# One float32 kernel of three layers: squares added on VectorE ahead of the norms' sums, v's norm scaled in another order, and short unread products in layer 2

## The chip, the core and the metric

The program runs on one core of one Trainium2 chip. The metric is the device time of one execution in microseconds, the median of the runs shown. Besides the timed runs one execution was profiled; its span runs from the first to the last instruction of the program.

## What is computed

Three different layers act one after the other on 1024 tokens with 1024 features, all in float32. Layer 1 is a chunkwise mLSTM with a pooling branch and a squared-ReLU MLP; layer 2 adds 16 meta tokens and runs a wide causal convolution beside an attention of 8 heads; layer 3 has a gated branch whose values are normed and mixed in chunks of 128 tokens, beside a gated linear attention. Cut to what the change touches:

```python
def layer_norm(x, g, b):                       # layer 1, after the mixer (norm 1)
    mu = xf.mean(-1, keepdims=True)
    var = jnp.square(xf - mu).mean(-1, keepdims=True)
    return ((xf - mu) * lax.rsqrt(var + LN_EPS) * g + b)

x = layer_norm(ALPHA * x + mix, ln1_g[l], ln1_b[l])
...
# layer 3: v is layer-normed over its 1024 features (a_ln_g, a_ln_b, eps 1e-6), then mixed over tokens
# layer 2: rms_norm of c_q and c_kv, queries, keys and values from them, then block-causal attention
```

## The kernel before, in words

**Layout.** Features lie on the 128 partitions in 8 rows of 1024 tokens, tokens along the free dimension. `res[:, m, :]` is row m of the residual, `M[g]` row g of v in layer 3. A mean over features is a sum over partitions and rows: `ones` (128x128) times a row, accumulated over the rows in a PSUM bank.

**Products.** Every large product splits both factors in a rounded part and a rest (`hi`, `lo`) and adds three products, hi·hi, hi·lo and lo·hi (L270 to L272 in `Core.product`, L324 to L326 in `Core.three`). One step of such a generator is three matmuls of 128x512. Weights come in tiles of 8 blocks: SyncE loads `w_raw`, ScalarE casts it to `w_hi` (`Core.cast`, L131), GpSimd subtracts to get `w_lo` (`Core.pool`, four instructions of 128x256 a tile), with three buffers each. A cast waits until TensorE has used up the tile three back.

**Order.** Nothing is scheduled by the hardware: each engine runs its own list of instructions in order and waits on semaphores. `Lane.settle` makes an engine wait for its own last instruction. `advance(fill, n)` puts n steps of a product between two steps of a norm on TensorE, and `label(name)` notes which products were finished by then. ScalarE and VectorE handle those products at the same names, with `act_products(name)` and `dve_products(name)`. So the place of such a call in an engine's list sets what stands behind the wait for that product.

**The norms.** `HalfNorm` norms 512 tokens at a time, u counting the halves: u = 0, 1 are norm 1 (after `w_out`, in `Ffn1.pe_norm`, `act_norm`, `dve_norm`), u = 2, 3 norm 2, u = 4, 5 the norm of v in layer 3 (`Mixer3.pe_sgu`, `act_sgu`, `dve_sgu`). The order is: TensorE sums `total`; ScalarE makes the mean; VectorE subtracts it from eight rows (`dve_centre`); ScalarE squares each row into one of two or three buffers (`act_square`); TensorE adds each square by `ones` in plain float32 (`pe_square`, one matmul instruction that the profile shows as two records); ScalarE makes Ln and Exp of the sum (`root_guess`); VectorE corrects by a Newton step (`root_newton`, four instructions) and scales the rows. In norm 1 the fill between two squares is 2 steps, and 5 steps come before the first. The fill of half 0 is the second half of `w_out` (64 steps, a product each 8), that of half 1 the first hidden rows of `w_ff1` (32 steps), whose squared ReLU goes to and fro between ScalarE and VectorE. In norm 1 VectorE centres all eight rows and only then handles the products that were finished during the squares. In v's norm the 16 squares have 2 steps between them, out of an 80-step fill (`lr`, `u3` 0, `s3` 0, `u3` 1, `s3` 1, 16 steps each); both halves' roots follow, then eight scalings of half 0, then of half 1, and ScalarE adds the shift to each and copies the turned v (`vt_ready`) after all sixteen.

**Layer 2's start** (`Mixer2.pe`): TensorE makes gate and a products and the latents c 3, 4, `rot`; sums for the rms of the keys' latents (`kv rms`); latents c 0 to 2; sums for the queries' (`q rms`); more gates; then values, keys and queries from the normed latents; then the first head's scores.

Of the kernel before, what the change touches and what calls it, by code (L numbers as in the profile page):

```python
# [441 lines left out]
class HalfNorm:  # L442


    def __init__(self, core):
        self.k = core
        s = core.s
        self.total, self.summed, self.mean = s("norm_total"), s("norm_summed"), s("norm_mean")
        self.centred, self.square, self.squares_summed = s("norm_centred"), s("norm_square"), s("norm_squares_summed")
        self.guess, self.scaled = s("norm_guess"), s("norm_scaled")  # L450

    def pe_sum(self, t, u, total):
        i = u % 2
# [8 lines left out]
    def act_mean(self, a, u, mean):  # L462
        a.wait_ge(self.summed, u + 1)
        a.act(mean, self.k.ps[:, 4 + u % 2, :], ACT.Copy, scale=1.0 / D, inc=self.mean)

    def act_square(self, a, u, k, x, squares):
        n = len(squares)
        a.wait_ge(self.centred, 8 * u + k + 1)
        a.wait_ge(self.squares_summed, 8 * u + max(k - n + 1, 0))
        a.act(squares[k % n], x, ACT.Square, inc=self.square)  # L470

    def dve_centre(self, v, u, k, x, mean):
# [1 line left out]
        v.tt(x, x, mean, ALU.subtract, inc=self.centred)  # L474

    def act_guess(self, a, u, root, eps):
        a.wait_ge(self.squares_summed, 8 * u + 8)
# [484 lines left out]
class Ffn1:  # L962
# [146 lines left out]
    def pe_norm(self, t, u, squares, fill, n, name):  # L1109

        i = u % 2
        self.norm.pe_sum(t, u, self.total[:, 512 * i:512 * i + 512])
        advance(fill, n[0])
        self.k.label(("sum " + name, i))
        advance(fill, n[1])
        self.k.label(("mean " + name, i))
        for c in range(8):
            advance(fill, n[1])
            self.k.label(("square " + name, i, c))
            self.norm.pe_square(t, u, c, squares[c % 3])  # L1120
        for c in range(8):
            advance(fill, n[2])
            self.k.label(("apply " + name, i, c))
# [99 lines left out]
    def act_norm(self, a, u, squares, mean, root, name, eps, apply):  # L1223
        i, cols = u % 2, slice(512 * (u % 2), 512 * (u % 2) + 512)
        self.norm.act_mean(a, u, mean)
        self.act_products(a, ("sum " + name, i))
        self.act_products(a, ("mean " + name, i))
        self.norm.act_square(a, u, 0, self.k.real(0)[:, cols], squares)
        for c in range(8):
            if c < 7:  # L1230
                self.norm.act_square(a, u, c + 1, self.k.real(c + 1)[:, cols], squares)
# [109 lines left out]
    def dve_norm(self, v, u, mean, root, tmp, name, gain, eps, split):  # L1341
# [4 lines left out]
        self.dve_products(v, ("mean " + name, i))  # L1346
        for c in range(8):
            self.norm.dve_centre(v, u, c, x(c), mean)
        for c in range(8):
            self.dve_products(v, ("square " + name, i, c))  # L1350
        v.settle()
        self.norm.dve_root(v, u, root, tmp, eps)
        self.norm.dve_scale(v, u, 0, x(0), gain, root)
# [83 lines left out]
class Mixer2:  # L1437
# [196 lines left out]
    def pe_ones(self, t, key, total, stream, value, inc):  # L1634
# [4 lines left out]
        t.wait_ge(stream, value)  # L1639
        t.mm(k.ones_of(total, THREE, range(p.first, p.first + 3)), inc)  # L1640

    def pe_in(self, t, key, cols):
        drain(self.k.product(t, key, [block_of("w_in_2", c, cols) for c in range(8)], self.k.hi, self.k.lo, THREE,
                             lambda c, i: [(self.ffn.x2_ready, (8 if i else 0) + c + 1)]))
        self.k.label(key)
# [196 lines left out]
    def pe(self, t):  # L1842
# [8 lines left out]
            self.pe_in(t, ("c", i), 1024 + i * P)  # L1851
        self.pe_in(t, ("rot",), [(64, 1664, 32), (96, 1680, 16), (112, 1664, 16)])
        self.pe_ones(t, ("kv rms",), self.comp_total, self.row_total, 1, self.rms_sum)
        for i in (0, 1, 2):
            self.pe_in(t, ("c", i), 1024 + i * P)
        self.pe_ones(t, ("q rms",), self.comp_total, self.row_total, 3, self.rms_sum)
        for c in (2, 3):
            self.pe_gate(t, c)
        advance(branch, self.early_taps())
        k.label("latents")  # L1860
        drain(self.pe_values(t))
        drain(self.pe_keys(t, 0))
        drain(self.pe_queries(t, 0))
        k.label("heads")
        for i in self.SCORE_AT.values():
            self.pe_score(t, 0, i)
        for p in range(3):
# [669 lines left out]
class Mixer3:  # L2537
# [116 lines left out]
    def pe_sgu(self, t):  # L2654
# [10 lines left out]
        self.norm.pe_sum(t, 5, self.total[:, 512:1024])  # L2665
        advance(fill, self.FILL_V)
        k.label("v3 sum")
        for u in (4, 5):
            advance(fill, self.FILL_NORM)
            k.label(("v3 mean", u))  # L2670
            for g in range(8):
                advance(fill, self.FILL_NORM)
                k.label(("v3 square", u, g))
                self.norm.pe_square(t, u, g, self.T[3 + g % 2][:, 0:512])
        advance(fill, 48 - self.FILL_TOTAL - self.FILL_V - 18 * self.FILL_NORM)
        k.label("v3 gate")
        advance(fill, 16)
        k.label("v3 normed")
        for g in range(8):
            vt = self.vt[g % 2]  # L2680
            for half in range(2):
                t.wait_ge(self.v_normed, 8 * half + g + 1)
                t.wait_ge(self.vt_ready, 2 * g + half - 1)
                t.mm([(ps[:, 6 + half, i * P:(i + 1) * P], self.M[g][:, (4 * half + i) * P:(4 * half + i + 1) * P], k.ident[:, :], True, True)
                      for i in range(4)], self.vt_turned, transpose=True)
# [134 lines left out]
    def act_sgu(self, a):  # L2820
        k, ps = self.k, self.k.ps
        self.act_products(a, "v3")
        for u in (4, 5):
# [2 lines left out]
                self.act_products(a, "v3 sum")  # L2826
            self.act_products(a, ("v3 mean", u))
            for g in range(8):
                self.norm.act_square(a, u, g, self.M[g][:, 512 * (u - 4):512 * (u - 3)], [self.T[3][:, 0:512], self.T[4][:, 0:512]])
                self.act_products(a, ("v3 square", u, g))  # L2830
        for u in (4, 5):
            self.norm.act_guess(a, u, self.root[:, 512 * (u - 4):512 * (u - 3)], EPS)
        for u in (4, 5):
            cols = slice(512 * (u - 4), 512 * (u - 3))
            for g in range(8):
                a.wait_ge(self.norm.scaled, 8 * u + g + 1)
# [149 lines left out]
    def dve_sgu(self, v):  # L2986
# [7 lines left out]
        for u in (4, 5):  # L2994
            cols = slice(512 * (u - 4), 512 * (u - 3))
            self.dve_products(v, ("v3 mean", u))
            for g in range(8):
                self.norm.dve_centre(v, u, g, self.M[g][:, cols], self.mean[:, cols])
                self.dve_products(v, ("v3 square", u, g))
        for u in (4, 5):  # L3000
# [3 lines left out]
            for g in range(8):  # L3004
                self.norm.dve_scale(v, u, g, self.M[g][:, cols], "a_ln_g_3", self.root[:, cols])
            if u == 4:
                self.dve_products(v, "v3 gate")
        self.dve_products(v, "v3 normed")
        for g in range(8):
            r = g % 2  # L3010
            self.dve_products(v, ("sgu", g))
# [474 lines left out]
```

## Time and profile before

| | us |
|---|---|
| median of 3 runs | 3557.8 (3557.28 to 3564.66) |
| the profiled execution, its own time | 3553.04 |
| its span | 3550.9 |
| granted TensorE clock, mean | 0.98 |

| engine | busy, us | share of the span |
|---|---|---|
| PE (TensorE matmul) | 3397.2 | 96% |
| PEld (weight loads) | 2781.4 | 78% |
| DVE (VectorE) | 1778.6 | 50% |
| ACT (ScalarE) | 1119.2 | 32% |
| POOL (GpSimd) | 1087.9 | 31% |

Times inside the execution are from the start of the span. Of the chain that ended last, 81% is on PE and 13% on DVE. The span's 2.1 us difference to the execution's own time lies outside the instructions. Norm 1 lies at 437 to 531 us, layer 2's start at 1290 to 1475, v's norm at 2732 to 2797. An entry of a timeline may merge several instructions of one kind (x8); an instruction can start before the one ahead of it has ended.

### The profile page before, as it was taken

What the parts mean: (1) busy time and instruction counts of PE and PEld (TensorE: products, weight loads), DVE (VectorE), ACT (ScalarE), POOL (GpSimd) and SP (SyncE); (2) the same over time, 40 slices, a digit from 0 to 9 for tenths busy, and PEclk for the clock granted to TensorE, in tenths of its full rate; (3) what the DMA queues carried; (4) which work ended last, traced back from release to release, by engine and by line L of the source; (5) the groups of instructions that cost most, each with busy time, mean ns of one, the idle gap of its engine ahead of it and who ended that gap; (6) DMA issues with size and microseconds to landing.
All of it is one profiled execution on the core that took longest, in us unless ns stands there. A gap on an engine that the chain in (4) does not pass through costs nothing.

```text
span 3550.9 us, 39250 instructions
## 1 busy us (share of the span) xinstructions
PE 3397.2 (96%) x16240; PEld 2781.4 (78%) x16240; DVE 1778.6 (50%) x1897; ACT 1119.2 (32%) x1493; POOL 1087.9 (31%) x1144
## 2 busy tenths in 40 slices
PE   8998999999999999898799999999999999999997
PEld 6665768888888688555499999999987788888776
DVE  4666563222223578777547546446474423444532
ACT  4443352111112532444533111111142533333442
POOL 3111344222333333100014334334334222222253
PEclk9999999999999999899899999999999999999998
DMA  3000311111111221000021111111113111011242
GB/s 126 24 26 28 107 66 64 49 48 48 48 48 49 71 90 36 24 7 7 6 78 42 48 48 48 48 48 44 48 41 110 51 66 54 30 36 35 78 142 95
DMA packets 56249, 192.21 MB, mean 54 GB/s; under 512 B 6900, under 2 KB 7284, under 8 KB 55560
## 3 DMA queue, kind: packets, MB, share of 16 engines
q1 hardware_dynamic: 56072, 189.71, 15.4%
q8 instruction: 128, 2.10, 0.2%
q14 instruction: 49, 0.40, 0.0%
HBM read 172.83 MB, written 16.86 MB: 53 GB/s over the span
## 4 chain that ended last, share of the span: by engine, by line
PE 81%; DVE 13%; ACT 4%; issue 1%; DMA 0%; POOL 0%; DVEq 0%; ACTq 0%; SPq 0%; POOLq 0%
PE psum L270 21%; PE psum L271 21%; PE psum L272 21%; PE psum L138 11%; DVE mix L107 3%; DVE work L98 2%; PE psum L324 2%; PE psum L325 2%; PE psum L326 2%; DVE res L98 1%; DVE softmax_shift_columns L113 1%; PE psum L136 1%; DVE u_padded L98 1%; ACT L126 1%; DVE res L107 1%
## 5 line engine op out<-in xcount | busy, mean ns | idle before, releaser
L98 POOL TENSOR_TENSOR w_lo<-w_raw,w_hi 128x256 fp32r<-128x256 f32 x1140 | 1087.7, 986 | 2428.2 <-ACT w_hi L131 2428.2
L270 PE MATMUL psum<-x_hi,w_hi 128*128 128x512 f32 (+2 forms) x3240 | 1200.7, 371 | 12.6 <-DVE mix L98 5.9
L271 PE MATMUL psum<-x_lo,w_hi 128*128 128x512 f32 (+2 forms) x3240 | 1165.0, 360 | 0.0
L272 PE MATMUL psum<-x_hi,w_lo 128*128 128x512 f32 (+2 forms) x3240 | 1161.4, 358 | 0.0
L131 ACT CAST w_hi<-w_raw 128x1024 fp32r<-128x1024 f32 x285 | 298.3, 1048 | 1509.9 <-PE psum L272 1436.9
L270 PEld LDWEIGHTS psum<-x_hi,w_hi 128*128 128x128 f32 x3240 | 612.7, 189 | 104.1 <-issue 20.7
L271 PEld LDWEIGHTS psum<-x_lo,w_hi 128*128 128x128 f32 x3240 | 612.3, 189 | 82.1 <-issue 17.5
L272 PEld LDWEIGHTS psum<-x_hi,w_lo 128*128 128x128 f32 x3240 | 610.6, 188 | 70.2
L270 PE MATMUL psum<-h_hi,w_hi 128*128 128x512 f32 x824 | 325.2, 395 | 3.1 <-DVE res L98 3.1
L272 PE MATMUL psum<-h_hi,w_lo 128*128 128x512 f32 x824 | 320.8, 389 | 0.0
L271 PE MATMUL psum<-h_lo,w_hi 128*128 128x512 f32 x824 | 320.7, 389 | 0.0
L107 DVE SCALAR_TENSOR_TENSOR res<-res,psum 128x1024 f32<-128x1024 f32 (+1 forms) x88 | 90.3, 1026 | 238.5 <-PE psum L272 229.3
L270 PEld LDWEIGHTS psum<-h_hi,w_hi 128*128 128x128 f32 x824 | 154.7, 188 | 37.8 <-DVE res L98 3.6
L271 PEld LDWEIGHTS psum<-h_lo,w_hi 128*128 128x128 f32 x824 | 154.7, 188 | 34.2 <-issue 2.6
L272 PEld LDWEIGHTS psum<-h_hi,w_lo 128*128 128x128 f32 x824 | 154.6, 188 | 32.3
L138 PE MATMUL psum<-res 128*65 128x256 f32 (+5 forms) x480 | 167.3, 433 | 8.0 <-ACT res L131 4.2
L98 DVE TENSOR_TENSOR h_tmp<-h_tmp 128x1024 f32<-128x1024 f32 (+1 forms) x36 | 55.1, 1532 | 237.5 <-ACT h_tmp L126 237.5
L107 DVE SCALAR_TENSOR_TENSOR mix<-u_padded,vectors,mix 128x1044 f32<-128x1044 f32 x120 | 168.6, 1405 | 5.0 <-ACT work L131 0.8
L98 DVE TENSOR_TENSOR up<-psum,ffn_rms 128x1026 f32<-128x1026 f32 x44 | 54.0, 1226 | 191.0 <-PE psum L272 189.3
L324 PE MATMUL psum<-x_hi,w_hi 128*128 128x348 f32 (+2 forms) x328 | 129.8, 396 | 18.2 <-DVE x_lo L98 9.0
L107 DVE SCALAR_TENSOR_TENSOR up_conv<-up,vectors,up_conv 128x1024 f32<-128x1024 f32 x88 | 143.7, 1633 | 3.1
L98 DVE TENSOR_TENSOR res<-res,psum 128x1024 f32<-128x1024 f32 (+1 forms) x56 | 68.5, 1224 | 140.8 <-PE psum L272 135.7
(281 smaller groups left out, 3727.2 us busy)
## 6 DMA issues: line engine op xcount, KB each, us to landing
w_raw<-w_dram SPq DMA_DIRECT2D x285, 512.0 KB, 3.2
res<-spill SPq DMA_DIRECT2D x4, 1044.0 KB, 9.6
res<-x_dram SPq DMA_DIRECT2D x8, 512.0 KB, 8.9
res<-x_dram SPq DMA_DIRECT2D x4, 1024.0 KB, 8.0
spill<-res SPq DMA_DIRECT2D x1, 4096.0 KB, 13.9
spill_a<-mix SPq DMA_DIRECT2D x8, 512.0 KB, 2.7
res<-spill_a SPq DMA_DIRECT2D x8, 512.0 KB, 4.6
x_plain<-spill SPq DMA_DIRECT2D x4, 1024.0 KB, 10.7
```

What stands on the lines that cost most here:

```text
L98: self.mark(self.e.tensor_tensor(out, a, b, op), inc)
L107: self.mark(self.e.scalar_tensor_tensor(out, a, s, b, op0, op1), inc)
L113: self.mark(self.e.tensor_reduce(out, a, AX.X, op, negate=negate), inc)
L126: self.mark(self.e.activation(out, a, func, bias=bias, scale=scale), inc)
L131: self.mark(self.e.copy(out, a), inc)
L138: ins = self.e.matmul(out, lhsT, rhs, start=start, stop=stop, skip_group_check=True)
L270: t.e.matmul(out, whi, xhi, start=k == 0, stop=False, skip_group_check=True)
L271: t.e.matmul(out, whi, xlo, start=False, stop=False, skip_group_check=True)
L272: ins = t.e.matmul(out, wlo, xhi, start=False, stop=last_k, skip_group_check=True)
L324: t.e.matmul(out, whi, xhi, start=first, stop=False, skip_group_check=True)
L325: t.e.matmul(out, whi, xlo, start=False, stop=False, skip_group_check=True)
L326: return t.e.matmul(out, wlo, xhi, start=False, stop=last, skip_group_check=True)
```

## The change

In norm 1 and v's norm (u = 0, 1, 4, 5) VectorE now adds squares into one row: seven adds in u = 0 and 4, so that TensorE sums once instead of eight times, and five adds in u = 1 and 5, so that it sums three times (`ADDED`). ScalarE writes the first square to the total's row and the others to two buffers. The adds stand between the centrings (`dve_add_square(c - 2)` behind centring c, from c = 3 on). In norm 1 the products finished during the squares are now handled between the centrings too, where all of them used to come after. The number of fill steps is the same; the sums stand behind all of that part's fill. In v's norm the sum of u = 4 stands among u = 5's fill (3 steps a row there), that of u = 5 at 54 steps instead of 46; 10 steps follow instead of 18. Ln and Exp of both halves are paired; both Newton steps come before any scaling; VectorE scales row by row, both halves of a row, each with a settle, and takes the fill's next product (`u3` 1) behind row 2. ScalarE takes `u3` 0 and `s3` 0 behind the Exps. In layer 2 `pe_idle` puts 16, 12, 12 and 12 matmuls of 128x128 in float32, whose result nobody reads, at four places: behind the `kv rms` sums, ahead of the `q rms` sums, ahead of the values, and ahead of the first scores.

```diff
 class HalfNorm:
+    ADDED = {0: 7, 1: 5, 4: 7, 5: 5}
+    def sums(self, u):
+        return sum(8 - self.ADDED.get(w, 0) for w in range(u))
+    def adds(self, u):
+        return sum(self.ADDED.get(w, 0) for w in range(u))
...
+    def pe_square_total(self, t, u, total, squares):
+        n = self.ADDED[u]
+        t.wait_ge(self.added, self.adds(u + 1))
+        t.mm([(self.k.ps[:, 6 + u % 2, :], self.k.ones[:, :], total, True, n == 7)], self.squares_summed)
+        for k in range(n + 1, 8):
+            self.pe_square(t, u, k, squares[k % 2])
+    def act_square_of(self, a, u, k, x, total, squares):
+        a.wait_ge(self.centred, 8 * u + k + 1)
+        a.wait_ge(self.squares_summed, self.sums(u))
+        a.wait_ge(self.added, self.adds(u) + max(k - 2, 0))
+        a.act(squares[k % 2] if k else total, x, ACT.Square, inc=self.square)
+    def dve_add_square(self, v, u, k, total, squares):
+        v.wait_ge(self.square, 8 * u + k + 1)
+        v.settle()
+        v.tt(total, total, squares[k % 2], ALU.add, inc=self.added)
...
@@ Ffn1.pe_norm
         for c in range(8):
             advance(fill, n[1])
             self.k.label(("square " + name, i, c))
-            self.norm.pe_square(t, u, c, squares[c % 3])
+        self.norm.pe_square_total(t, u, squares[2], squares)
@@ Ffn1.dve_norm
         for c in range(8):
             self.norm.dve_centre(v, u, c, x(c), mean)
-        for c in range(8):
-            self.dve_products(v, ("square " + name, i, c))
+            if c > 2:
+                self.norm.dve_add_square(v, u, c - 2, self.squares[2], self.squares)
+            if c:
+                self.dve_products(v, ("square " + name, i, c - 1))
+        self.dve_products(v, ("square " + name, i, 7))
+        for c in range(6, self.norm.ADDED[u] + 1):
+            self.norm.dve_add_square(v, u, c, self.squares[2], self.squares)
@@ Mixer2
+    def pe_idle(self, t, n):
+        for _ in range(n):
+            t.e.matmul(self.k.ps[:, 6, 0:P], self.k.ones[:, :], self.k.ident[:, :], start=True, stop=True, skip_group_check=True)
...
         self.pe_ones(t, ("kv rms",), self.comp_total, self.row_total, 1, self.rms_sum)
+        self.pe_idle(t, 16)
         for i in (0, 1, 2):
             self.pe_in(t, ("c", i), 1024 + i * P)
+        self.pe_idle(t, 12)
         self.pe_ones(t, ("q rms",), self.comp_total, self.row_total, 3, self.rms_sum)
...
         k.label("latents")
+        self.pe_idle(t, 12)
...
         k.label("heads")
+        self.pe_idle(t, 12)
@@ Mixer3.pe_sgu
             for g in range(8):
-                advance(fill, self.FILL_NORM)
+                advance(fill, self.FILL_NORM + u - 4)
                 k.label(("v3 square", u, g))
-                self.norm.pe_square(t, u, g, self.T[3 + g % 2][:, 0:512])
-        advance(fill, 48 - self.FILL_TOTAL - self.FILL_V - 18 * self.FILL_NORM)
+                if u == 5 and g == 2:
+                    self.norm.pe_square_total(t, 4, self.T[3][:, 512:1024], squares)
+        self.norm.pe_square_total(t, 5, self.T[4][:, 512:1024], squares)
         k.label("v3 gate")
-        advance(fill, 16)
+        advance(fill, 64 - self.FILL_TOTAL - self.FILL_V - 18 * self.FILL_NORM - 8)
...
-                t.wait_ge(self.v_normed, 8 * half + g + 1)
+                t.wait_ge(self.v_normed, 2 * g + half + 1)
@@ Mixer3.act_sgu
+        for i, cols in enumerate(halves):
+            a.wait_ge(self.norm.squares_summed, self.norm.sums(5 + i))
+            a.act(self.root[:, cols], ps[:, 6 + i, :], ACT.Ln, bias=k.tiny[:, 1:2], scale=1.0 / D)
+        a.settle()
+        for cols in halves:
+            a.act(self.root[:, cols], self.root[:, cols], ACT.Exp, scale=-0.5, inc=self.norm.guess)
+        self.act_products(a, "v3 gate")
...
@@ Mixer3.dve_sgu
                 self.norm.dve_centre(v, u, g, self.M[g][:, cols], self.mean[:, cols])
+                if g > 2:
+                    self.norm.dve_add_square(v, u, g - 2, self.T[u - 1][:, 512:1024], [self.T[3][:, 0:512], self.T[4][:, 0:512]])
                 self.dve_products(v, ("v3 square", u, g))
...
             self.norm.dve_root(v, u, self.root[:, cols], self.tmp[:, cols], EPS)
-            for g in range(8):
+        self.dve_products(v, "v3 gate")
+        for g in range(8):
+            for u in (4, 5):
+                cols = slice(512 * (u - 4), 512 * (u - 3))
+                v.settle()
                 self.norm.dve_scale(v, u, g, self.M[g][:, cols], "a_ln_g_3", self.root[:, cols])
-            if u == 4:
-                self.dve_products(v, "v3 gate")
-        self.dve_products(v, "v3 normed")
+            if g == 2:
+                self.dve_products(v, "v3 normed")
```

## Rows read from the trace of the kernel before

**Rows 1.** The page: busy time, share and instructions of the engines.
```profile
PE 3397.2 (96%) x16240; PEld 2781.4 (78%) x16240; DVE 1778.6 (50%) x1897; ACT 1119.2 (32%) x1493; POOL 1087.9 (31%) x1144
```

**Rows 2.** Timeline, PE, norm 1 half 0: start, duration, instruction, idle before.
```profile
442.91 1.02 PE L138 MATMUL psum<-h_plain,ones 128*128 128x512 f32 x2
...
444.47 0.39 PE L270 MATMUL psum<-x_hi,w_hi 128*128 128x512 f32 x1
444.70 0.39 PE L271 MATMUL psum<-x_lo,w_hi 128*128 128x512 f32 x1
...
445.16 1.02 PE L138 MATMUL psum<-h_plain,ones 128*128 128x512 f32 x2
```

**Rows 3.** Timeline, DVE, norm 1: centrings, half 0's last `w_out` product, a hidden row's rest.
```profile
439.00 5.50 DVE L98 TENSOR_TENSOR res<-res,h_plain 128x512 f32<-128x512 f32 x8 [1.92 <-ACT h_plain L126]
...
489.47 0.69 DVE L107 SCALAR_TENSOR_TENSOR res<-res,psum 128x512 f32<-128x512 f32 x1 [0.50 <-PE psum L272]
...
510.74 1.15 DVE L98 TENSOR_TENSOR h_lo<-h_tmp,h_hi 128x512 fp32r<-128x512 f32 x1 [0.68 <-ACT h_hi L131]
```

**Rows 4.** Timeline, DVE, 466 to 474 us, beside the POOL tile of rows 5.
```profile
470.74 1.23 DVE L98 TENSOR_TENSOR x_lo<-res,x_hi 128x512 fp32r<-128x512 f32 x1
```

**Rows 5.** Timeline, POOL, 434 to 545 us: a weight tile.
```profile
468.38 4.18 POOL L98 TENSOR_TENSOR w_lo<-w_raw,w_hi 128x256 fp32r<-128x256 f32 x4 [10.62 <-ACT w_hi L131]
```

**Rows 6.** Timeline, ACT, norm 1: Ln of half 0, a cast, Ln of half 1.
```profile
459.74 0.69 ACT L126 ACTIVATE h_plain<-psum,tiny 128x512 f32<-128x512 f32 x1 [3.12 <-PE psum L138]
...
507.58 1.05 ACT L131 CAST w_hi<-w_raw 128x1024 fp32r<-128x1024 f32 x1 [2.31 <-PE psum L272]
...
513.56 0.69 ACT L126 ACTIVATE h_plain<-psum,tiny 128x512 f32<-128x512 f32 x1 [1.02 <-PE psum L138]
```

**Rows 7.** Windows, PE: stretch, its length, busy (instructions), granted clock, DMA share, GB/s.
```profile
525.80:531.00 5.20, 5.20 (x12) 0.50 0.22 79
...
2790.00:2795.00 5.00, 3.84 (x21) 1.00 0.01 3
```

**Rows 8.** Waits of PE, 1270 to 1480 us, the longest four: total, times, longest.
```profile
PE psum L270 <- DVE mix L98: 5.3, 1, 5.3
PE psum L374 <- DVE x_lo L98: 3.9, 1, 3.9
PE psum L138 <- DVE work L98: 3.9, 1, 3.9
PE psum L138 <- ACT x_hi L131: 3.4, 1, 3.4
```

**Rows 9.** Windows, PE, behind the four holes of layer 2; columns as in rows 7.
```profile
1335.20:1339.90 4.70, 4.70 (x16) 0.50 0.12 49
...
1375.80:1380.90 5.10, 5.07 (x11) 0.50 0.30 103
...
1429.90:1435.50 5.60, 5.60 (x13) 0.50 0.28 94
...
1456.10:1473.00 16.90, 13.52 (x38) 0.50 0.00 0
```

**Rows 10.** Timeline, DVE, 1378 to 1390 us: VectorE after the queries' rms sums.
```profile
1384.58 1.25 DVE L98 TENSOR_TENSOR work<-squares 128x1044 f32<-128x1044 f32 x1 [2.84 <-ACT squares L126]
```

**Rows 11.** Timeline, PE, v's norm: its last square, and the first chunk mixing.
```profile
2776.56 1.02 PE L138 MATMUL psum<-res,ones 128*128 128x512 f32 x2
...
2797.06 2.05 PE L138 MATMUL psum<-res,work 128*128 128x128 f32 x16 [0.82 <-ACT work L131]
```

**Rows 12.** Timeline, DVE, v's norm half 1: Newton step's start, eight scalings.
```profile
2787.26 0.69 DVE L98 TENSOR_TENSOR work<-res 128x512 f32<-128x512 f32 x1
...
2789.91 5.39 DVE L107 SCALAR_TENSOR_TENSOR mix<-mix,vectors,res 128x512 f32<-128x512 f32 x8
```

**Rows 13.** Timeline, ACT, v's norm half 0: the table load between Ln and Exp.
```profile
2775.84 1.28 ACT L126 ACT_TABLE_LOAD   x1
```

More of the change, by code:

```diff
@@ L450, in __init__ @@
         self.guess, self.scaled = s("norm_guess"), s("norm_scaled")
+        self.added = s("norm_square_added")
     def pe_sum(self, t, u, total):
@@ L468, in act_square @@
         a.wait_ge(self.centred, 8 * u + k + 1)
-        a.wait_ge(self.squares_summed, 8 * u + max(k - n + 1, 0))
+        a.wait_ge(self.squares_summed, self.sums(u) + max(k - n + 1, 0))
         a.act(squares[k % n], x, ACT.Square, inc=self.square)
@@ L476, in act_guess @@
     def act_guess(self, a, u, root, eps):
-        a.wait_ge(self.squares_summed, 8 * u + 8)
+        a.wait_ge(self.squares_summed, self.sums(u + 1))
         self.k.root_guess(a, root, self.k.ps[:, 6 + u % 2, :], D, eps, self.guess)
@@ L1227, in act_norm @@
         self.act_products(a, ("mean " + name, i))
-        self.norm.act_square(a, u, 0, self.k.real(0)[:, cols], squares)
+        self.norm.act_square_of(a, u, 0, self.k.real(0)[:, cols], squares[2], squares)
         for c in range(8):
             if c < 7:
-                self.norm.act_square(a, u, c + 1, self.k.real(c + 1)[:, cols], squares)
+                self.norm.act_square_of(a, u, c + 1, self.k.real(c + 1)[:, cols], squares[2], squares)
             self.act_products(a, ("square " + name, i, c))
@@ L2667, in pe_sgu @@
         k.label("v3 sum")
+        squares = [self.T[3][:, 0:512], self.T[4][:, 0:512]]
         for u in (4, 5):
@@ L2828, in act_sgu @@
             for g in range(8):
[L2829 to L2834, printed above, removed]
-            for g in range(8):
-                a.wait_ge(self.norm.scaled, 8 * u + g + 1)
+                self.norm.act_square_of(a, u, g, self.M[g][:, 512 * (u - 4):512 * (u - 3)], self.T[u - 1][:, 512:1024],
+                                        [self.T[3][:, 0:512], self.T[4][:, 0:512]])
+                if u == 4:
+                    self.act_products(a, ("v3 square", u, g))
+                else:
+                    k.cast(a, k.at["v3 square", u, g][0])
+        halves = [slice(0, 512), slice(512, 1024)]
+        for i, cols in enumerate(halves):
[6 more added lines that the diff above has]
+        for g in range(8):
+            for i, cols in enumerate(halves):
+                a.wait_ge(self.norm.scaled, 32 + 2 * g + i + 1)
                 a.act(self.M[g][:, cols], self.M[g][:, cols], ACT.Identity, bias=k.column("a_ln_b_3", g), inc=self.v_normed)
@@ L2998, in dve_sgu @@
                 self.norm.dve_centre(v, u, g, self.M[g][:, cols], self.mean[:, cols])
+                if g > 2:
+                    self.norm.dve_add_square(v, u, g - 2, self.T[u - 1][:, 512:1024], [self.T[3][:, 0:512], self.T[4][:, 0:512]])
                 self.dve_products(v, ("v3 square", u, g))
+            for g in range(6, self.norm.ADDED[u] + 1):
+                self.norm.dve_add_square(v, u, g, self.T[u - 1][:, 512:1024], [self.T[3][:, 0:512], self.T[4][:, 0:512]])
         for u in (4, 5):
@@ L3003, in dve_sgu @@
             self.norm.dve_root(v, u, self.root[:, cols], self.tmp[:, cols], EPS)
-            for g in range(8):
+        self.dve_products(v, "v3 gate")
+        for g in range(8):
+            for u in (4, 5):
+                cols = slice(512 * (u - 4), 512 * (u - 3))
+                v.settle()
                 self.norm.dve_scale(v, u, g, self.M[g][:, cols], "a_ln_g_3", self.root[:, cols])
-            if u == 4:
-                self.dve_products(v, "v3 gate")
-        self.dve_products(v, "v3 normed")
+            if g == 2:
+                self.dve_products(v, "v3 normed")
         for g in range(8):
```

## The prediction

> **What bounds the kernel.** The page comes first: PE is busy for 96% of the span [rows 1], so work taken from TensorE counts one for one, unless another engine's chain takes its place where it stood. So next I read, for each edited stretch, the timelines of PE, DVE and ACT side by side and ask who is waited for at its end. In norm 1 half 0 TensorE goes without a pause: square, two fill steps, square [rows 2]. ScalarE's Ln waits for it [rows 6], VectorE has long centred all rows [rows 3]. TensorE is the bound there and VectorE has slack; the question is how much of it 7 or 5 adds use up. In layer 2 the list of PE's waits gives four holes of 5.3, 3.9, 3.9 and 3.4 us [rows 8], and the windows behind them show a granted clock of 0.50, which is 1.2 GHz instead of 2.4 [rows 9].
>
> **Prices.** Records of the split products start 0.23 us apart (444.47, 444.70), so a step of three takes 0.68. From square to square 2.25 us pass, of which two steps are 1.36: one square's sum costs 0.89 [rows 2]. The change drops 7 + 5 + 7 + 5 = 24 of them, 21.4 us of PE work. A centring takes 5.50 / 8 = 0.69 us [rows 3]; an add of the same shape, which waits for its own engine, I take at 0.72. Beside a working GpSimd the same form takes 1.23 [rows 4], and a weight tile's four subtractions last 4.2 us then [rows 5], so a tile costs a busy VectorE about 4 x 0.5 = 1.8 to 2 us.
>
> The Trainium skill says so too (GPSIMD Engine Reference, Key points): GpSimd shares its SBUF interfaces with VectorE and contends with instructions that have two SBUF inputs, as all the adds have. Without it half 0 below would end its adds about 3.5 us sooner.
>
> **Norm 1, half 0: about +1.0.** Without squares TensorE reaches the sum 8 x 0.89 = 7.1 us before 459.6, where it now ends the squares [rows 6], so at 452.5. VectorE: `dve_products("square", 1)` stands behind centring 2 and waits for the fill's first product, 13 steps before 452.5, at 443.7. Centrings 3 to 6 and adds 1 to 4 stand behind that wait: 444.4 + 4 x 1.38 + 1.8 for the tile cast meanwhile = 451.7. Then product 1 (0.69 + 0.72), long done: 453.1. Then centring 7 and adds 5, 6, 7: 2.9 + 1.2 for the next tile = 457.1. TensorE waits 4.6 us, sums once (0.89) and is 1.6 us ahead of before. But a wait of this size lowers the clock: behind norm 1's present one 5.2 us were granted 0.50 [rows 7], which costs half, 2.6. TensorE's fill ends the half (VectorE waits for its last product, 489.47 [rows 3]), so the half ends at -1.6 + 2.6 = +1.0.
>
> **Norm 1, half 1: about +5.4.** TensorE arrives at 513.7 - 7.1 = 506.6. The first hidden row is done 13 steps earlier, 497.8. From its cast's start to the end of its rest 4.3 us pass (507.58 to 511.89 [rows 3, 6]): 502.1. Only then centring 3; four pairs at 1.38 give 507.6; then square 6 (0.6), because ScalarE's list has it ahead of the second row, then that row's cast and ping-pong, 4.3: 512.5. Centring 7 and add 5: 513.9. TensorE has waited 7.2 us, and the three sums left run at the low clock, 3 x 1.75 = 5.2: Ln at 519.1 instead of 513.56 [rows 6]. The 11 steps, the roots and the pair of rows behind it follow at their old distances. What waits behind these stalls: ScalarE's casts of product 1's tile (3 to 5 us late, used two products of 5.5 us later), so POOL's `w_lo` and SyncE's loads of `w_raw`, which follow the casts; three buffers cover that. Without that cover TensorE would wait the same 3 to 5 us.
>
> **V's norm: about +1.3.** Half u = 4 fits: its adds end some 3 us before TensorE's step 39. In u = 5 VectorE waits for `s3` 0 (step 48). PE's squares now end at 2777.5 [rows 11]; two steps more and 15 sums fewer put that product near 2764.2. Then 1.2 for it, two centrings and two adds, 2.8, and 1.3 for its tile: 2769.5. TensorE arrives at 2767.9 and ends three sums at 2772.2. Ln 0.7, table load 1.28 [rows 13], Exp 0.6: 2774.8. Two Newton steps, each 2789.91 - 2787.26 = 2.65: 2780.1. Sixteen scalings, now each settled, at 0.79 instead of 5.39 / 8 = 0.67 [rows 12]: 12.6, with `u3` 1 among them 1.25: 2793.9. ScalarE's last shift 0.8 and two copies 1.05: the chunk mixing starts at 2795.8 instead of 2797.06 [rows 11], -1.3. TensorE now stands idle for 8.7 us before it, so again 2.6 for the clock. So 10.7 us of sums are gone and 1.3 us of time is lost. Unchanged work behind it is TensorE's alone.
>
> Between Ln and Exp the row shows a table load [rows 13]. The Trainium skill (ScalarE: Activation LUTs, Table sets) has a set with both functions; by that rule the load would not be there and v's norm would come out 1.3 us lower. The trace decides; I count the load.
>
> **Layer 2: about -9.3.** A short float32 matmul costs 2.05 / 8 = 0.26 us [rows 11]: 16 are 4.1, 12 are 3.1. They fit into holes of 5.3, 3.9, 3.9 and 3.4 and leave 1.2, 0.8, 0.8 and 0.3 idle [rows 8]; a stretch with 1.2 us idle kept its 1.00 [rows 7]. So the clock should hold. If the cover went, they would cost 13.5 us. The low stretches [rows 9] return half: 4.7 / 2 = 2.4 on PE up to c 2, then `q rms` 1.9, which VectorE takes up because it idles 2.84 for it [rows 10] and is busy from there to the values, then 5.6 / 2 = 2.8. That is 7.1 to 7.3. For the scores I take 2.0, between 0 (their stretch is 3.4 us idle in 16.9, the clock may fall anyway) and 4: VectorE's maxima set the pace for its first ten microseconds.
>
> **Sum.** 1.0 + 5.4 + 1.3 - 9.3 = -1.6 on the profiled execution (span 3550.9, own time 3553.0). The median is 4.8 above that; I carry the difference: 3557.8 - 1.6 = **3556.2**.
>
> **Rivals.** (1) *The new waits leave the clock alone.* Then half 0 gives -1.6, half 1 +2.8, v's norm -1.3, layer 2 -9.3: -9.4, 3548.4. Against it: every hole over 3 us in rows 8 has its low stretch. (2) *Contention stays away* (VectorE, streaming, keeps GpSimd out): half 0 ends its adds at 453.6 and needs no clock; -5.1 instead of +1.0: -7.7, 3550.1. (3) *The adds are hidden altogether*, as slack in DVE (50% busy) suggests: -21.4 - 9.3 = -30.7, 3527. Against it: the position of the products between the centrings. (4) *Slower: the short matmuls do not hold the clock.* They are short and each reloads its weights; if the windows behind the holes stay at 0.50, layer 2 gives nothing and the norms' +7.7 stand alone: 3565.5. It decides from three of the four holes on. This is also the case in which a part does not do what it says.
>
> The Trainium skill speaks against the norms' part (TensorE: Matmul & The Clock Gate, HAM oscillation): idle gaps behind which TensorE starts cold are paid each time. Rows 7 and 9 agree with it; by that rule rival 1 is out.
>
> **Chances.** Forecast 0.50 (own range 3551 to 3562), rival 1 0.17, rival 2 0.13, rival 3 0.06, rival 4 0.14. About 0.2% (7 us) is what a measurement of this kernel tells from no change. Faster by more: rival 1 at 0.15, half of rival 2, rival 3: 0.28. Slower by more: two thirds of rival 4, the upper end of the forecast: 0.12. Within: 0.60. The range leaves out rival 3 and the outer ends: 3545 to 3566.
>
> **What will show it.** PE's waits at norm 1: "DVE h_plain" of about 4.6 and 7 us ahead of the sums, windows at 0.50 behind them; Ln of half 1 about 6 us later after its sum than now; PE's wait for ACT ahead of v's mixing near 8 us; windows behind layer 2's holes at 1.00 and the stretch from 1290 to 1475 some 9 us shorter. It is wrong if the adds follow the squares without a wait, if the clock stays at 1.00 behind the new waits, or at 0.50 behind the short matmuls.

## The result and the profile after

| | before | after |
|---|---|---|
| median, us | 3556.2 (3553.11 to 3564.66) | 3560.1 (3558.15 to 3568.43) |
| profiled execution, own time | 3553.04 | 3559.28 |
| its span | 3550.9 | 3557.5 |

The kernel became slower: the ratio is 1.0016 with an interval of 1.0010 to 1.0022, which is +5.7 us (+3.6 to +7.8); the two medians differ by 3.9, and the runs of either kernel spread over some 10 us. The forecast was -1.6 us on the profiled execution; that execution shows +6.2. The time after lies inside the range, but on the other side of the time before.

The page of after first, in the columns of [rows 1]:

```profile
PE 3391.6 (95%) x16296; PEld 2786.9 (78%) x16296; DVE 1800.5 (51%) x1921; ACT 1119.5 (31%) x1492; POOL 1087.7 (31%) x1144
```

TensorE is busy for 5.6 us less than in [rows 1] and the span is 6.6 us longer. So the work was taken away and came back as waiting, and as work at the lower clock. The weight casts tell where: both kernels cast the same 285 tiles, and the start of a cast in after less its start in before gives a shift at each place. It moves by a few us in stretches that nobody edited: it is -0.9 at 430 us, and it grows by 1.7 between 3301 and 3402 us. So only its change across an edited stretch is read, in us. How far to trust it shows in the runs below that leave a stretch unedited: there the change is at most 0.4 in layer 2's start and 0.1 in v's norm, but in norm 1 it is +0.3 in two runs and +2.1 to +2.3 in three. The norm 1 line is therefore good to some 2 us, the other two to some tenths.

| stretch | predicted | after | that part alone (experiment 1) |
|---|---|---|---|
| norm 1 (430 to 560) | +6.4 | +5.4 | +5.8 |
| layer 2's start (1279 to 1479) | -9.3 | -3.7 | -3.7 |
| v's norm (2728 to 2830) | +1.3 | +4.5 | +4.4 |
| sum | -1.6 | +6.2 | +6.5 |

The three +2 changes in norm 1 all arise behind one wait, at the start of half 1, of 2.08 or 2.09 us. In `v_only` the clock stays up behind that same wait, in `fills_long` it falls; the kernel before waits 1.51 us there, at 1.00. `v_only` first, then `fills_long`:

```profile
492.00:498.00 6.00, 6.00 (x24) 1.00 0.46 160
```

```profile
492.00:498.00 6.00, 6.00 (x18) 0.72 0.47 163
```

**Norm 1.** PE's waits from 440 to 535 us, the longest (total, times, longest), and then what PE did at both; they answer to [rows 2]:

```profile
PE psum L138 <- DVE h_plain L98: 13.3, 2, 8.6
```

```profile
456.48 1.93 PE L138 MATMUL psum<-h_plain,ones 128*128 128x512 f32 x2 [4.76 <-DVE h_plain L98]
...
514.26 4.73 PE L138 MATMUL psum<-h_plain,ones 128*128 128x512 f32 x6 [8.57 <-DVE h_plain L98]
```

TensorE now waits 4.76 and 8.57 us for the adds. A sum that took 1.02 us in [rows 2] takes 1.93 behind the first wait, since the granted clock is 0.50. VectorE's timeline in half 0, against [rows 3], shows why:

```profile
438.14 2.49 DVE L98 TENSOR_TENSOR res<-res,h_plain 128x512 f32<-128x512 f32 x3 [1.92 <-ACT h_plain L126]
442.92 0.69 DVE L107 SCALAR_TENSOR_TENSOR res<-res,psum 128x512 f32<-128x512 f32 x1 [2.29 <-PE psum L272]
443.53 0.69 DVE L98 TENSOR_TENSOR res<-res,h_plain 128x512 f32<-128x512 f32 x1
444.32 1.13 DVE L98 TENSOR_TENSOR h_plain<-h_plain 128x512 f32<-128x512 f32 x1
445.38 1.22 DVE L98 TENSOR_TENSOR res<-res,h_plain 128x512 f32<-128x512 f32 x1
...
453.12 3.31 DVE L98 TENSOR_TENSOR h_plain<-h_plain 128x512 f32<-128x512 f32 x3
```

Three centrings, 2.29 us of waiting for the fill's product, and only then centring 3 and add 1. Each add and centring takes 1.1 to 1.2 us while GpSimd makes a tile, as in [rows 4], and 0.69 otherwise.

**V's norm.** PE's waits from 2735 to 2815 us. In before this list has no wait over 1.2 us:

```profile
PE psum L138 <- ACT work L131: 7.6, 1, 7.6
PE psum L136 <- ACT mix L126: 2.8, 1, 2.8
PE psum L138 <- DVE res L98: 2.5, 1, 2.5
```

**Layer 2.** Windows of PE behind the four holes of after (columns as in rows 7), to be laid beside [rows 9]:

```profile
1339.50:1344.20 4.70, 4.64 (x19) 0.64 0.10 42
1379.50:1384.60 5.10, 5.10 (x27) 1.00 0.29 103
1431.40:1437.00 5.60, 4.87 (x14) 0.70 0.30 96
1457.20:1474.00 16.80, 12.88 (x39) 0.59 0.00 1
```

All four were at 0.50. One is at 1.00 now; the other three lie between 0.59 and 0.70, so they are low for a part of their time.

### The profile page after: what moved, and what is told of

The parts are those of the page before. It is cut to its first block, busy times and chain, and to the rows that moved or that the text cites. A ratio compares the mean times of both kernels' runs of the same rounds, so it can differ in the third digit from the quotient of the medians.

```text
span 3557.5 us, 39408 instructions
## 1 busy us (share of the span) xinstructions
PE 3391.6 (95%) x16296; PEld 2786.9 (78%) x16296; DVE 1800.5 (51%) x1921; ACT 1119.5 (31%) x1492; POOL 1087.7 (31%) x1144
## 4 chain that ended last, share of the span: by engine, by line
PE 81%; DVE 14%; ACT 4%; issue 1%; DMA 0%; POOL 0%; DVEq 0%; ACTq 0%; SPq 0%; POOLq 0%
PE psum L270 21%; PE psum L271 21%; PE psum L272 21%; PE psum L138 10%; DVE mix L107 3%; DVE work L98 2%; PE psum L324 2%; PE psum L326 2%; PE psum L325 2%; DVE res L98 1%; DVE softmax_shift_columns L113 1%; PE psum L136 1%; DVE u_padded L98 1%; DVE mix L98 1%; ACT L126 1%
## 5 line engine op out<-in xcount | busy, mean ns | idle before, releaser
L271 PEld LDWEIGHTS psum<-x_lo,w_hi 128*128 128x128 f32 x3240 | 612.6, 189 | 76.8 <-issue 10.7
```

Of the source, the lines that this page charges most:

```text
L271: t.e.matmul(out, whi, xlo, start=False, stop=False, skip_group_check=True)
```

## The experiments

Each is the kernel before with the edit named, unless said otherwise. A comparison has the ratio of its runs to those of the kernel before on the same chip; a change of shift across a stretch comes from the profiled execution, and where both are given the second is the finer measure, because it leaves out what other stretches did. But it compares single executions, and that of the kernel before, 3553.04, is among its fastest.

**1. The three parts alone.** `norm1_only` has the changes of `HalfNorm` and of `Ffn1`, `v_only` those of `HalfNorm` and of `Mixer3`, `fills_only` has `pe_idle`. No other edit.

> Norm 1's part alone, the rest as before. Theory from the two traces (effects are local, each stretch keeps what it lost or gained up to the end): +5.5 us over the kernel before, because TensorE waits 4.7 and 8.6 us for VectorE's adds and is granted 0.50 behind both waits. By the prediction's terms it would be +6.4. Rival (a later stretch absorbs the delay, because something other than TensorE sets its end, a transfer or VectorE): under +2.

Measured 1.0014 (1.0005 to 1.0023), +5.0 us; shift across norm 1 +5.8. The waits are those of after, 13.3 us in two.

> The part of v's norm alone. Theory from the traces: +4.5 us, made of 1.8 (the chunk mixing starts later against TensorE's work before it) and 2.7 (granted clock 0.50 behind the two long waits). By the prediction's term it would be +1.3. Rival (the low clock of the run of after at 2795 belonged to that run, as some low stretches move between executions): about +1.8, and windows at 1.00 behind the waits.

Measured 1.0008 (0.9999 to 1.0016), +2.8 us, which by itself does not exclude no change; shift +4.4, with the same three waits of 7.6, 2.8 and 2.5.

> Layer 2's short products alone. Theory from the traces: -3.7 us, with the windows behind three of the four holes still at 0.50 for 3.4 us or more. By the prediction's term it would be -9.3. Rival (the low stretches of after came from its execution, not from the gaps that are left): windows at 1.00 behind three holes and about -9.

Measured 0.9985 (0.9976 to 0.9994), -5.3 us; shift -3.7, and the windows of after once more:

```profile
1339.60:1344.30 4.70, 4.68 (x20) 0.66 0.13 52
1379.50:1384.60 5.10, 5.06 (x27) 1.00 0.30 103
1431.50:1437.10 5.60, 4.88 (x13) 0.70 0.30 97
1457.40:1474.30 16.90, 13.14 (x40) 0.60 0.00 1
```

So the effects are local, those of the edited stretches repeat from execution to execution, and by the shifts they add up: 5.8 + 4.4 - 3.7 = 6.5 against 6.2 for the whole. The ratios are too coarse to confirm it: 5.0 + 2.8 - 5.3 = 2.5 against 5.7, each part known to 3 us. Nothing later takes a delay back. All three rivals of these runs fall.

**2. Longer fills in layer 2.**

```diff
-        self.pe_idle(t, 16)
+        self.pe_idle(t, 23)
...
-        self.pe_idle(t, 12)
+        self.pe_idle(t, 17)    # behind c 0 to 2
...
-        self.pe_idle(t, 12)
+        self.pe_idle(t, 19)    # ahead of the values
...
-        self.pe_idle(t, 12)
+        self.pe_idle(t, 15)    # ahead of the scores
```

> Layer 2's short products alone, with 23, 17, 19 and 15 of them instead of 16, 12, 12 and 12, at 0.23 us each: of the gaps of 1.78, 1.27, 1.76 and 0.77 us that after shows behind them, about 0.1 to 0.2 us is left. Theory A (what is left of a gap decides the clock): the windows behind holes a and c go to 1.00, TensorE gains 1.7 in hole a and some 2 in c more than in the kernel with the shorter fills: about -7 in all. Theory B (short products do not keep the clock however many): low stretches as with the shorter fills, -3.7 again, or worse where a fill overruns its hole, by up to 0.5 each.

Measured 0.9979 (0.9970 to 0.9987), -7.5 us; shift across the stretch -6.8 instead of -3.7. The windows behind the same holes:

```profile
1337.50:1342.20 4.70, 4.52 (x28) 1.00 0.16 61
1376.00:1381.10 5.10, 5.04 (x27) 1.00 0.34 103
1428.00:1433.60 5.60, 4.88 (x20) 1.00 0.29 94
1452.40:1469.30 16.90, 13.09 (x40) 0.60 0.00 0
```

At the first three holes the clock does what theory A says, and theory B falls. By the shifts at the holes' ends the first two give 2.3 + 2.0 us, where the prediction had 2.4 + 1.9. The third disappoints in another way. The clock is 1.00 there, yet it gives 1.9 us and not 2.8, since TensorE comes for VectorE's rows of `x_lo` sooner than they are ready, 0.22 + 0.67:

```profile
1428.05 0.47 PE L374 MATMUL psum<-w_hi,x_hi 128*128 128x512 f32 x1 [0.22 <-DVE x_lo L98]
...
1429.65 0.50 PE L374 MATMUL psum<-w_hi,x_hi 128*128 128x512 f32 x1 [0.67 <-DVE x_lo L98]
```

The fourth stretch falls to the lower clock even with its hole filled. TensorE goes on waiting for VectorE's maxima there, four times and 2.6 us in all.

**3. Norm 1 with the fill's products behind the roots** (on top of `norm1_only`):

```diff
-            self.act_products(a, ("square " + name, i, c))
+            self.k.cast(a, self.k.at["square " + name, i, c][0])
...
-            if c:
-                self.dve_products(v, ("square " + name, i, c - 1))
-        self.dve_products(v, ("square " + name, i, 7))
```

> Norm 1's part alone, with the fill's products handled behind the roots instead of between the centrings, on VectorE and ScalarE, for both halves (the weight casts stay where they were). Theory (what holds the adds back is the wait for the fill's product between them, and its ping-pong with ScalarE): half 0's adds follow from 440.7 on, 5 centrings and 7 adds at 0.7 and some contention end them near 451, before TensorE arrives at 452; in half 1 they end by 502, before 506. No wait ahead of the sums, Ln 6 us sooner in half 0 and some 4 in half 1; against that the products come later. So between -3 and -11.6 (12 sums of 0.89 and nothing lost), likeliest -7 against the kernel before. Rival (the number of adds and the contention with GpSimd set their end, wherever the products stand): waits of 3 us and more stay, the time is that of the part alone, about +5.

Measured 0.9987 (0.9978 to 0.9996), -4.6 us; shift across norm 1 -4.7 instead of +5.8. The adds' wait shrinks from 13.3 us to 0.4; but new ones stand behind it. PE's waits, 435 to 535 us:

```profile
PE psum L324 <- POOL w_lo L98: 5.1, 1, 5.1
PE psum L138 <- DVE total L98: 3.4, 2, 1.9
PE psum L324 <- ACT h_tmp L126: 2.6, 1, 2.6
PE psum L270 <- DVE res L107: 1.4, 1, 1.4
PE psum L138 <- DVE h_plain L98: 0.4, 1, 0.4
```

The same number of adds, beside the same GpSimd, is hidden as soon as no product stands between the centrings. That settles it: the place of the products makes the loss, not the number of adds. Of the 10.7 us of sums 4.7 arrive as time. The new waits for a weight tile (5.1) and a bank (2.6) stand in half 1, where the hidden rows' products come late now; that they take the rest is argued from this list, not tested.

**4. Norm 1 with TensorE kept at work in its waits** (on top of `norm1_only`):

```diff
         n = self.ADDED[u]
+        for _ in range({0: 18, 1: 34}.get(u, 0)):
+            t.e.matmul(self.k.ps[:, 6 + u % 2, 0:P], self.k.ones[:, :], self.k.ident[:, :], start=True, stop=True, skip_group_check=True)
```

> Norm 1's part alone, with 18 and 34 short products of 0.23 us each on TensorE ahead of its waits for the adds, which leaves 0.7 and 0.9 us of 4.8 and 8.6 idle. They only keep TensorE at work. Theory: the granted clock stays at 1.00 behind both; of the part's +5.5 the clock's share is what TensorE did at 0.50 behind them, 3.4 us in half 0 and 3.9 in half 1, halved 3.6: about +2. By the prediction's terms the clock's share would be 2.6 and 2.6. Rival (the granted clock behind such waits has no part in the loss because VectorE and ScalarE set the end of each half): +5.

Measured 1.0002 (0.9993 to 1.0011); shift across norm 1 +2.7 instead of +5.8. First `norm1_only` behind its two waits, then this kernel:

```profile
457.60:461.00 3.40, 3.38 (x6) 0.50 0.50 157
515.60:519.50 3.90, 3.90 (x5) 0.50 0.28 107
```

```profile
457.50:460.00 2.50, 2.50 (x9) 1.00 0.38 102
...
514.50:518.00 3.50, 3.50 (x10) 1.00 0.33 129
```

The clock's share of the loss is 5.8 - 2.7 = 3.1 us by these two executions, where the prediction had 2.6 in each half. The runs' ratios give 5.0 - 0.7 = 4.3, with 3 us of uncertainty in each. So that the clock has a part is shown by the windows, and its size is known roughly.

**5. V's norm, half 4's sum earlier, and `s3` 0 behind the adds** (on top of `v_only`):

```diff
-                if u == 5 and g == 2:
+                if u == 5 and g == 0:
...
-                self.dve_products(v, ("v3 square", u, g))
+                if u == 4 or g < 5:
+                    self.dve_products(v, ("v3 square", u, g))
...
+        self.dve_products(v, ("v3 square", 5, 7))      # behind the adds of half 5
```

> The part of v's norm alone, with half 4's sum on TensorE at the first of half 5's steps instead of the third (6 steps, 4.1 us sooner) and s3 0 handled by VectorE behind the adds of half 5. Theory (ScalarE's first square of half 5 waits for that sum, 2754.2 to 2758.5, and pushes the adds behind it): the adds end about 4 us sooner, TensorE's wait of 2.5 us for them is gone and the clock does not fall before the three sums: Ln 3 us sooner, the mixing too: +1 instead of +4.5 for the part. Rival (VectorE's own work, 23 us of centrings and adds beside GpSimd, sets the end): +4.

Measured 0.9998 (0.9989 to 1.0007); shift across v's norm +1.1 instead of +4.4. ScalarE's timeline at the first square of half 5, first of after, then of this kernel:

```profile
2758.52 0.63 ACT L126 ACTIVATE res<-mix 128x512 f32<-128x512 f32 x1 [4.69 <-PE psum L138]
```

```profile
2757.72 0.63 ACT L126 ACTIVATE res<-mix 128x512 f32<-128x512 f32 x1 [1.65 <-PE psum L138]
```

In after ScalarE stands for 4.69 us until TensorE has summed half 4: `act_square_of` waits for `squares_summed` of the half before. All squares of half 5, and VectorE's adds, come behind that. Here this wait is 1.65. TensorE now waits 0.78 us ahead of half 4's early sum, and ahead of half 5's three sums, where it waited 2.50, not at all. They take 2.74 us instead of 4.38:

```profile
2771.80 2.74 PE L138 MATMUL psum<-res,ones 128*128 128x512 f32 x6
```

The run makes two edits at once. The adds end at 2768.4, and `s3` 0, handled ahead of them as before, would make that some 2769.6 (1.2 us for the product), still ahead of TensorE's 2771.8. So by this estimate the earlier sum is enough; no run has it alone.

**6. V's norm with ScalarE's copies of row 0 early** (on top of `v_only`):

```diff
                 a.act(self.M[g][:, cols], self.M[g][:, cols], ACT.Identity, bias=k.column("a_ln_b_3", g), inc=self.v_normed)
+            if g == 2:
+                self.act_turned_v(a, 0)     # the two copies of row 0
         for g in range(8):
-            for half in range(2):
...                                         # its two waits and the copy
+            if g:
+                self.act_turned_v(a, g)
```

> The part of v's norm alone, with ScalarE's two copies of the turned row 0 behind its sixth shift instead of behind all sixteen. Theory (TensorE's 7.6 us of waiting before the mixing and the 10.2 us at 0.50 behind it come from the copies' place in ScalarE's list, which the scaling row by row does not use): mixing 0 starts near 2792 instead of 2799, the part comes out at about +4.5 - 7 - 2.7 = -5. Rival (VectorE, which has ten scalings left at that time and the products and biases behind them, is waited for next): the wait moves to VectorE, gain under 3, about +2.

Measured 0.9976 (0.9967 to 0.9985), -8.5 us; shift across v's norm -5.3 instead of +4.4. TensorE's wait of 7.6 us for the copies is 0.7, and behind it the clock is whole:

```profile
PE psum L138 <- ACT work L131: 0.7, 1, 0.7
```

```profile
2794.00:2805.00 11.00, 11.00 (x63) 1.00 0.00 0
```

In after the same eleven microseconds, 2794 to 2805, have 5.73 us of work at 0.54. The change scales row by row, and TensorE turns row 0 as soon as it is ready; but ScalarE takes up the turned row only behind its sixteenth shift.

**7. All of it together.** `combined` is after with the edits of 2, 3, 5 and 6.

> The whole change with what four runs showed: in norm 1 the fill's products behind the roots, in v's norm half 4's sum at the first of half 5's steps, s3 0 behind the adds and ScalarE's copies of row 0 behind the sixth shift, in layer 2 fills of 23, 17, 19 and 15. Theory (the parts add up, since each stretch hands its gain on to the end unchanged): norm 1 -4.7, v's norm +4.4 - 3.4 - 9.7 = -8.7, layer 2 -6.8, in all -20 us against the kernel before, some 3536. Rival (in v's norm the two cures overlap, because VectorE's 16 scalings and the products behind them are waited for once the copies come early): v's norm -5.3 and no more, -17 in all.

Measured 0.9942 (0.9929 to 0.9956), a median of 3537.5 against 3557.8: -20.3 us. That is the -20 of the theory, but not by its terms. By shifts norm 1 gives -5.6, layer 2 -3.5 instead of -6.8, and v's norm -8.5, in all -17.6; the profiled execution is 15.6 us below that of the kernel before, which is one of its fastest. So the total fits in part by luck. The two cures in v's norm do not overlap. Layer 2 gives as much as alone up to the scores (-6.3), and loses 2.8 in them, where the longer fills alone gained 0.5. The clock stays low through the scores for longer: 20 us at 0.50, where the longer fills alone had 14 at 0.51. First this kernel, then `fills_long`:

```profile
1449.00:1469.00 20.00, 17.75 (x47) 0.50 0.00 0
```

```profile
1455.00:1469.00 14.00, 11.51 (x35) 0.51 0.00 0
```

Why it does is not shown: TensorE's waits for the maxima are nearly the same in both, 2.8 us in four and 2.6 in four. `combined_rows_first` moves norm 1's products once more, on VectorE as shown and on ScalarE likewise:

```diff
+        if u == 0:
+            self.dve_products(v, ("square " + name, i, 7))
...
-            self.dve_products(v, ("apply " + name, i, c))
+            if u == 0 or c > 3:
+                self.dve_products(v, ("apply " + name, i, c))
```

> As the combined kernel, but in norm 1 half 0's products stand right behind the adds and half 1's behind the fourth row of the normed half, on VectorE and ScalarE. Theory (in norm 1 with late products TensorE's new wait of 5.1 us stands behind a weight tile that ScalarE casts only after the products' ping-pong of 7 us, and a wait of 1.4 us in half 0 behind a bank that VectorE frees late): both waits shrink, 3 to 5 us less than the combined kernel. Rival (the rows' own chain of two roots and eight rows sets the end of half 1): the same time within 1.5 us.

Measured 0.9953 (0.9940 to 0.9965), 3540.1 us: no gain over `combined`, as far as their intervals tell; across norm 1 the shift is -3.9 where `combined` had -5.6. The 3 to 5 us of the theory are out. The rival's time is not excluded, but its reason is not what the trace shows. The two waits, 2.6 and 5.1 us, did not shrink but became one of 10.2:

```profile
527.47 0.77 PE L324 MATMUL psum<-x_hi,w_hi 128*128 128x512 f32 x1 [10.18 <-ACT h_tmp L126]
```

TensorE's next products need a bank that only ScalarE's ReLU of the first hidden row frees, and that ReLU stands behind four rows now. Neither of the two theories had named the bank. The wait of 1.4 us in half 0 is gone, as expected.

## Why the prediction was wrong, point by point

**Bound, and the method.** That TensorE sets the end and each stretch hands on what it gained or lost was right; the parts alone show it. Both waits that were forecast for norm 1 are there, and the wait for ACT ahead of v's mixing near 8 us is 7.6. The steps that failed are two, in v's norm and in layer 2.

**Norm 1: the mechanism right, +6.4 against +5.4, two sizes off.** The execution came into this stretch 0.9 us early. Half 0: TensorE arrives at 451.7 (452.5 forecast), the adds end at 456.4 (457.1), the wait is 4.76 (4.6). Half 1: the wait is 8.57 (7.2). The Ln starts at 519.03, 5.5 us later than in before and 6.3 later with the 0.9 added; 1.0 + 5.5 was forecast:

```profile
519.03 0.69 ACT L126 ACTIVATE h_plain<-psum,tiny 128x512 f32<-128x512 f32 x1 [2.80 <-PE psum L138]
```

The mechanism is shown by experiment 3. One term was too large, the clock: 3.1 us by experiment 4 (4.3 by the ratios) and not 5.2 [rows 7]. In after the clock falls while TensorE still stands idle (a mean of 0.62 from 506 to 514 us, without any work), and is whole again some 4 us behind each wait, not 5.2. What falls on idle time costs nothing. Half 0 ends at -0.1 against its start, and not at +1.0. The wait of half 1 was too small by 1.4 us. These two errors go against each other, so that the sum comes so near is in part luck, and this is the stretch whose shift is good to 2 us only.

A sum of the prediction is off here without consequence: half 0's adds without contention would end 1.8 + 1.2 = 3.0 us sooner by its own terms, not 3.5.

**V's norm: +4.5 against +1.3, wrong by 3.2.** The step that failed is "half u = 4 fits: its adds end some 3 us before TensorE's step 39". It is true (they end at 2754.2), and it looked at the wrong party. I asked whether TensorE would wait for the adds of half 4, and not who waits for the sum. ScalarE does, for 4.69 us, ahead of half 5's first square. VectorE reached `s3` 0 at 2765.9 and not at 2764.2, the adds ended at 2771.1 and not at 2769.5, and TensorE's wait for them was 2.5 us and not 1.6. The prediction had given this wait no low clock, and it got one:

```profile
2771.18 4.38 PE L138 MATMUL psum<-res,ones 128*128 128x512 f32 x6 [2.50 <-DVE res L98]
```

Three sums took 4.4 instead of 2.7 us. The mixing starts at 2799.3 instead of 2795.8. Of these 3.5 us the execution brought 0.5 along from earlier; some 0.9 are the longer wait, 1.7 the slower sums, and 0.3 TensorE's own later arrival. With the 3.0 of the stretch itself the prediction's sum becomes -1.3 + 3.0 + 2.7 = +4.4. Everything behind the sums ran as forecast: two Newton steps 5.2 (5.3), the scalings with `u3` 1 among them 13.9 (13.85), 2.7 for the clock behind the wait (2.6). With the sum moved and `s3` 0 behind the adds (experiment 5) the part costs +1.1, near what the prediction gave it.

One reading was right although its sum is not: 2777.5 with two steps more (1.4) and 15 sums fewer (13.4) is 2765.5 and not 2764.2. TensorE had `s3` 0 ready at 2764.6, 0.5 late like all of this stretch, so 2764.2 was met, and VectorE's later 2765.9 is not the product's doing.

The table load stands between Ln and Exp in after as well:

```profile
2776.31 1.28 ACT L126 ACT_TABLE_LOAD   x1
```

So the row decides against the rule of the Trainium skill (ScalarE: Activation LUTs, Table sets) for this kernel: to count the load was right.

**Layer 2: -3.7 against -9.3, wrong by 5.6, the larger miss.** The step that failed is "So the clock should hold". Either miss alone would have turned the sign of -1.6: this one to +4.0, that of v's norm to +1.6. (The terms of -9.3 add up to 9.1; its 7.3 is the upper end of "7.1 to 7.3".) Hole by hole, a gain being the shift at the hole's end less that at the next hole's end:

| hole | short products | left, forecast | left, after | gain, forecast | gain, after | gain, longer fills |
|---|---|---|---|---|---|---|
| a, up to c 2 | 16 | 1.2 | 1.78 | 2.4 | 0.7 | 2.3 |
| b, `q rms` | 12 | 0.8 | 1.27 | 1.9 | 2.0 | 2.0 |
| c, the values | 12 | 0.8 | 1.76 + 0.67 | 2.8 | 0.5 | 1.9 |
| d, the scores | 12 | 0.3 | 0.77 | 2.0 | 0.4 | 0.5 |

Two terms lie behind this. One was the price of a short product. I took it from the mixing, 2.05 / 8 = 0.26 [rows 11]; it is 3.73 / 16 = 0.23:

```profile
1334.05 3.73 PE L1679 MATMUL psum<-identity,ones 128*128 128x128 f32 x32
```

So some 0.4 to 0.5 us more was left idle in each hole (16 or 12 times 0.03). The row that I rested the rest on, 1.2 us idle at 1.00 [rows 7], was met in hole b, and there the clock held and the whole gain came. In hole c 1.76 us were left, 0.5 more than the price explains; that TensorE came earlier there, having gained in b what VectorE had not, is an inference. The other is that half of a low stretch was counted as gain. Holes c and d have VectorE as their pace: in c TensorE meets the next `x_lo`, in d the maxima. For d the prediction had said so and taken 2.0 between 0 and 4; it is 0.5. For c I had not looked at who is waited for next. With fills of the right length the stretch gives -6.8, and the 2.5 that are missing to -9.3 are nearly all those two, 0.9 in c and 1.5 in d.

**The rivals.** Rival 4 (the short products do not hold the clock) came nearest by its time, +7.7 against +6.2 on the profiled execution, but not by its mechanism: the longer fills held it, and the norms' part came out at 9.9 instead of 7.7. Its sign, 0.50 behind the short matmuls, was half there: three of four windows were low for a part of their time. Rivals 1, 2 and 3 are out: the clock fell behind both waits in norm 1, the adds took 1.2 us beside GpSimd, and 13.3 us of waiting stood where rival 3 had none. The Trainium skill's rule that the change had against it (TensorE: Matmul & The Clock Gate, HAM oscillation) agrees with the windows at 0.50 behind the norms' waits; its price here, 3.1 us in norm 1, is from experiment 4 and is rough.

**What stays open.** Why the shift between 3301 and 3402 us grows by 1.4 to 2.2 us in after and five of the experiments, by 0.8 in three and not at all in two: a low stretch differs in length there, in code that no edit touches. Why the clock falls in three of five executions behind the same wait of 2.1 us at the start of norm 1's half 1. Why the low stretch in layer 2's scores is longer in `combined`. How much of the adds' time is GpSimd's doing, which experiment 3 shows only to be small enough to hide. Whether the clock could be held through the first scores wasn't tried.

## What to carry to other kernels

When partial sums move to another engine, follow the queue of every engine that shares a semaphore with them: here the loss did not come from the adds, but from a product handled between two centrings, from a square that waits for the other half's sum, and from two copies behind sixteen shifts; each was a call or two in an engine's list, and together with the longer fills their cures turned +5.7 us into -20.3. Fill a hole with work that is priced by its own record, and count as gain only what the next engine in line does not take. A wait is dear twice where TensorE is the bound, by itself and by the clock behind it, but the clock costs only in so far as its low stretch falls on work.

## What the runs showed of the hardware that was not expected

Short float32 products of 128x128 run at 0.23 us each, and where they fill a wait the granted clock is 1.00 behind it, even though nobody reads them: in `norm1_clock` 34 in a row, 7.75 us, stood in front of a window at 1.00, where `norm1_only` without them had 0.50.

Behind idle gaps of nearly the same length the clock can go either way. In after the 2.79 us ahead of v's turned row are followed by 0.57, and in the kernel with the early sum, where the wait before them had gone, the same 2.79 us are followed by 1.00:

```profile
2784.00:2788.00 4.00, 2.83 (x11) 0.57 0.00 0
```

```profile
2783.50:2787.50 4.00, 3.23 (x17) 1.00 0.00 0
```

The wait of 2.1 us at the start of norm 1's half 1 says the same, in code that these runs leave alone: the clock stays at 1.00 behind it in two executions and falls in three (windows in the section on the result). So a gap's length alone, read from one row, was too little for the forecast that the clock would hold.
